# Single decay matrix in the delta-rule preparation, a block-by-block second half of the output projection, and modulation rows around the first attention steps

## The reference, cut to what matters

```python
mod = silu(c) @ w_mod + b_mod                       # 6 rows of 1024: shift, scale, gate, twice
h = rms_norm(x, pre_mix_gain) * (1 + scale_m) + shift_m
y = hybrid_mixer(h, ...)                            # proj = h @ w_in; two head groups; concat @ w_out
x = x + gate_m * rms_norm(y, post_mix_gain)
h = rms_norm(x, pre_ffn_gain) * (1 + scale_f) + shift_f
y = peer_ffn(h, ...)                                # product keys, top 16, 16384 experts
x = x + gate_f * rms_norm(y, post_ffn_gain)
```

```python
gdiff = g[:, None] - g[None, :]                     # g: cumulated log decay
decay = where(incl, exp(gdiff), 0)
L     = where(strict, (k * beta) @ k.T * decay, 0)  # strictly lower
sol   = triangular_solve(I + L, [v*beta, k*beta*exp(g)])
qk    = q @ k.T * decay
```

## Time and profile before

| | us |
|---|---|
| median of 3 runs | 1740.15 (1738.11 to 1740.58) |
| the profiled execution | 1740.75, span 1738.9 |
| PE busy | 1680.7, 97% of the span |
| DVE busy | 1245.3, 72% |
| POOL busy | 905.1, 52% |
| ACT busy | 701.5, 40% |

### The profile page before, as it was taken

One profiled execution on the slowest core, in us unless ns is written; L12 is line 12 of the kernel. 1 busy time (PEld: TensorE's weight loads), 2 busy tenths in 40 slices (PEclk: granted clock), 3 DMA queues, 4 the chain that ended last, 5 costly groups with the idle time before them and its releaser, 6 DMA issues.

```text
span 1738.9 us, 25635 instructions
## 1 busy us (share of the span) xinstructions
PE 1680.7 (97%) x7938; PEld 1393.7 (80%) x7938; DVE 1245.3 (72%) x3050; ACT 701.5 (40%) x1044; POOL 905.1 (52%) x710
## 2 busy tenths in 40 slices
PE   6999979987999999999999999999999999999997
PEld 5777769976888888888888888888888888888886
DVE  7658877584139999899899522223888888888886
ACT  5454565534233444444444444333333333333333
POOL 0232302043330177778777877761676776767730
PEclk9999989998999999999999999999999999999999
DMA  9422393353225644444444444466999999999993
GB/s 353 176 82 74 117 418 132 122 216 111 85 91 174 214 146 145 146 146 145 145 146 145 145 145 145 135 228 225 337 345 372 358 376 367 359 377 350 380 342 140
DMA packets 149363, 376.21 MB, mean 216 GB/s; under 512 B 32048, under 2 KB 64944, under 8 KB 146096
## 3 DMA queue, kind: packets, MB, share of 16 engines
q1 hardware_dynamic: 114480, 308.04, 50.0%
q0 software_dynamic: 34816, 67.41, 10.8%
HBM read 312.25 MB, written 63.11 MB: 216 GB/s over the span
## 4 chain that ended last, share of the span: by engine, by line
PE 90%; DVE 6%; ACT 2%; issue 1%; DVEq 1%; DMA 0%; SPq 0%; ACTq 0%
PE bank L1095 16%; PE bank L1096 16%; PE bank L1097 16%; PE bank L1494 10%; PE bank L1498 10%; PE bank L1496 10%; PE bank L1111 1%; PE bank L1113 1%; PE bank L1112 1%; PE bank L1295 1%; PE bank L1310 1%; PE bank L1454 1%; DVE modr L1568 1%; DMA xn<-in_x 0%; PE bank L1320 0%
## 5 line engine op out<-in xcount | busy, mean ns | idle before, releaser
L661 POOL DMA_INDIRECT gate_scratch<-merged,idx_cell x384 | 433.0, 1128 | 212.3 <-issue 125.3
L1095 PE MATMUL bank<-act_hi,whi 128*128 128x512 f32 x1312 | 514.5, 392 | 0.4 <-DVE act_lo L1590 0.4
L1096 PE MATMUL bank<-act_lo,whi 128*128 128x512 f32 x1312 | 511.1, 390 | 0.0
L1097 PE MATMUL bank<-act_hi,wlo 128*128 128x512 f32 x1312 | 511.1, 390 | 0.0
L1983 DVE TENSOR_TENSOR wlo<-raw,whi 128x1024 fp32r<-128x1024 f32 x254 | 309.9, 1220 | 180.2 <-ACT whi L1009 178.6
L1494 PE MATMUL bank<-whi,chi 128*128 128x512 f32 x768 | 298.8, 389 | 0.0
L1496 PE MATMUL bank<-wlo,chi 128*128 128x512 f32 x768 | 298.8, 389 | 0.0
L1498 PE MATMUL bank<-whi,clo 128*128 128x512 f32 x768 | 298.8, 389 | 0.0
L1095 PEld LDWEIGHTS bank<-act_hi,whi 128*128 128x128 f32 x1312 | 246.9, 188 | 51.6 <-DVE act_lo L1590 1.1
L1097 PEld LDWEIGHTS bank<-act_hi,wlo 128*128 128x128 f32 x1312 | 246.6, 188 | 51.5
L1096 PEld LDWEIGHTS bank<-act_lo,whi 128*128 128x128 f32 x1312 | 246.8, 188 | 50.1
(11 more groups left out here) (323 smaller groups left out, 1833.4 us busy)
## 6 DMA issues: line engine op xcount, KB each, us to landing
raw<-in_expert_tiles SPq DMA_DIRECT2D x256, 512.0 KB, 4.0
act_scratch<-aout SPq DMA_DIRECT2D x128, 256.0 KB, 2.1
gate_scratch<-zeros SPq DMA_DIRECT2D x24, 1024.0 KB, 22.4
a_in<-act_scratch SPq DMA_DIRECT2D x128, 192.0 KB
g_in<-gate_scratch SPq DMA_DIRECT2D x128, 192.0 KB, 7.0
raw<-in_in_tiles SPq DMA_DIRECT2D x28, 512.0 KB, 3.4
modr<-in_mod_tiles SPq DMA_DIRECT2D x16, 512.0 KB, 12.1
modz<-in_mod_tiles SPq DMA_DIRECT2D x16, 512.0 KB, 6.9
```

Of the source, the lines that this page charges most:

```text
L661: g.indirect_dma_start(out=gate_cells, out_offset=bass.IndirectOffsetOnAxis(ap=idx_cell[:, b, k:k + 1], axis=0), in_=merged[:, b, k:k + 1] ...
L1095: mm(out_bank[:], whi[:, slot, w], act_hi[:, k, :], start=(k == 0), stop=False)
L1096: mm(out_bank[:], whi[:, slot, w], act_lo[:, k, :], start=False, stop=False)
L1097: last = mm(out_bank[:], wlo[:, slot, w], act_hi[:, k, :], start=False, stop=(k == KD - 1))
```

## The change

Three parts.

1. Modulation rows 24 to 39 move to the front: 24 to 33 (`EARLY = 34`) right behind `gate_columns(0)`, then two in each of attention steps 0, 1 and 2, between biased(s) and difference(s). SP issues four rows ahead of each of tiles 8 to 13, with a wait only for the row that used the slot. The buffers `modz` are gone.
2. Delta-rule preparation: only `QKT` is built and passed through `Exp`; `a_products` multiplies it by the grams into `LM`, PE transposes that (`a_transposes`), and `first_level` multiplies by beta. The spread copy `gB` goes: PE reads the decay column as a broadcast operand. norm_sums(0..3) stand one tile earlier; the last V tile is copied by ACT to `state`, and its convolution stands behind the first masks. Four `qk_normed` stand in the first doubling steps.
3. Output projection: tiles 32 to 35 get slots of their own for every second pair, and their products run block by block: all 48 matmuls of block 0, then block 1, 2, 3. The chain of each block (root, gate, add, square, root, scale) follows on ACT and DVE; POOL adds nothing any more.

The names in the next two pieces: `modx`, `modr` are slots of modulation rows, `modcol` their results, `mrow` holds the lambda sums, `baT` the decay and beta columns.

The diff, cut to its core:

```diff
+EARLY = 34
...
-                if 26 <= m < 40:
-                    sp.wait_ge(s_uw, NB)
-                if 32 <= m < 40:
+                if 8 <= m < 40:
                     sp.wait_ge(s_modu, m - 7)
...
             for n in range(T_KQ, T_OUT):
-                for m in range(2 * n, min(2 * n + 2, 24)):
+                for m in range(4 * n - 16, min(4 * n - 12, 40)):
                     load_mod(m)
                 load_raw(n, in_tiles[n])
...
# DVE, start of attention
             gate_columns(0)
+            for m in range(24, EARLY):
+                mod_tile(m)
...
+                for m in range(EARLY + 2 * s, min(EARLY + 2 * s + 2, 40)):
+                    mod_tile(m)
...
# PE, preparation
-                if s == H * NB + 1:
+                if s == H * NB:
                     for n2 in range(4):
                         norm_sums(n2)
...
+            decay_rows(0)
             norm_sums(4)
...
+            decay_rows(1)
...
+            decay_rows(2)
+            norm_sums(5)
+            norm_sums(6)
+            pe.wait_ge(s_v3, 1)
+            decay_rows(3)
+            norm_sums(7)
...
# DVE, preparation
-                for out, m, ready in ((LM, M_NOT_STRICT, s_du[0]), (QKT, M_NOT_U, s_du[1])):
-                    for h in range(H):
...
+                for h in range(H):
+                    last = stt(out=QKT[:, t, h * HD:(h + 1) * HD], in0=row[:, h, :],
...
+            def a_products(t):
+                dve.wait_ge(s_kg, t + 1)
+                dve.wait_ge(s_de, t + 1)
+                tt(LM[:, t, :], QKT[:, t, :], bank[4 + t][:], ALU.mult).then_inc(s_A, 1)
+
+            def first_level(t):
+                dve.wait_ge(s_AT, t + 1)
+                tt(by_head(LM[:, t, :]), by_head(bank[t][:]), bc(g16(G_BETA), t), ALU.mult).then_inc(s_L, 1)
...
             first_masked(NB - 1)
+            dve.wait_ge(s_v3, 1)
+            conv(11)
+            v.drain()
+            v.memset(state[:], 0.0).then_inc(s_st, 1)
...
# PE, second half of the output projection
+            for b in range(NB):
+                for q in range(4):
+                    n = T_OUT + 4 + q
+                    h, l = out_weights(n)
+                    if b == 0:
+                        split_wait(n)
+                    for kk in range(2):
...
# DVE, behind it
+            for b in range(NB):
+                if b >= 1:
+                    x1_mean(b - 1)
                 block_mean(b)
+                y_by_gate(b, 1)
+                if b >= 1:
+                    x1_root(b - 1)
                 block_root(b)
+                stt(out=xn[:, b, :], in0=xs2[:, b, :], scalar=rstd[:, b:b + 1], in1=xn[:, b, :],
+                    op0=ALU.mult, op1=ALU.add).then_inc(s_x1[b], 1)
```

More of the change, by code:

```diff
@@ L841, in _ @@
                         sc.activation(l2r[:, n, :], qkvT[:, n, :], ACT.Square).then_inc(s_sq, 1)
-            for n in range(8):
-                act.wait_ge(s_l2, n + 1)
-                sc.activation(l2r[:, L2_ORDER[n], :], bank[SUM_BANK[n]][:], ACT.Ln,
-                              bias=eps_t).then_inc(s_l2r, 1)
+            for n in range(4):
+                norm_log(n)
+            act.wait_ge(s_used, T_OUT)
+            sc.copy(state[:], bank[1][:]).then_inc(s_v3, 1)
+            for n in range(4, 8):
+                norm_log(n)
             def inverse_norm(n):
@@ L854, in _ @@
             for t in range(NB):
-                act.wait_ge(s_du[0], t + 1)
-                sc.activation(LM[:, t, :], LM[:, t, :], ACT.Exp, scale=-1.0).then_inc(s_de, 1)
-            for n in range(4, 8):
-                inverse_norm(n)
-            act.wait_ge(s_du[1], NB + 1)
+                act.wait_ge(s_du, t + 1)
+                sc.activation(QKT[:, t, :], QKT[:, t, :], ACT.Exp).then_inc(s_de, 1)
+            act.wait_ge(s_du, NB + 1)
             for t in range(NB):
@@ L862, in _ @@
             last.then_inc(s_de, 1)
-            for t in range(NB):
-                sc.activation(QKT[:, t, :], QKT[:, t, :], ACT.Exp)
             sc.activation(g16(G_EXP), g16(G_CUM), ACT.Exp)
@@ L1342, in join_t @@
                 last.then_inc(s_tt, 1)
+            for t in range(NB):
+                a_transposes(t)
+            for t in range(NB):
+                first_transposes(t)
             for n in range(6 * NB + 1):
@@ L1733, in _ @@
             v.tensor_copy(g16(G_CUM), bank[7][:, 0:16]).then_inc(s_gcc, 1)
-            v.memset(state[:], 0.0).then_inc(s_st, 1)
             v.drain()
@@ L1738, in _ @@
                 row = by_head(bank[ROW_BANK[t]][:])
-                for out, m, ready in ((LM, M_NOT_STRICT, s_du[0]), (QKT, M_NOT_U, s_du[1])):
-                    for h in range(H):
-                        last = stt(out=out[:, t, h * HD:(h + 1) * HD], in0=row[:, h, :],
-                                   scalar=g16(G_CUM)[:, 4 * t + h:4 * t + h + 1], in1=masks[:, m, :],
-                                   op0=ALU.subtract, op1=ALU.add)
-                    last.then_inc(ready, 1)
+                for h in range(H):
+                    last = stt(out=QKT[:, t, h * HD:(h + 1) * HD], in0=row[:, h, :],
+                               scalar=g16(G_CUM)[:, 4 * t + h:4 * t + h + 1], in1=masks[:, M_NOT_U, :],
+                               op0=ALU.subtract, op1=ALU.add)
+                last.then_inc(s_du, 1)
                 tt(g16(G_DEC)[:, 4 * t:4 * t + 4], row[:, :, CH - 1], g16(G_CUM)[:, 4 * t:4 * t + 4],
@@ L1786, in first_masked @@
                 masked(t)
-            for n in range(6):
+            for n in range(4):
                 qk_normed(n)
+            for t in range(NB):
+                a_products(t)
             for t in range(NB):
@@ L1817, in _ @@
                 updated(n)
+                if n < 4:
+                    qk_normed(4 + n)
                 if n in QK_STEPS:
@@ L1903, in block_root @@
                 v.drain()
-            def y_gated(b):
-                for half in range(2):
-                    w = slice(half * 512, (half + 1) * 512)
-                    last = stt(out=xs2[:, b, w], in0=bank[4 * half + b][:], scalar=rstd[:, b:b + 1],
-                               in1=gate_m[:, w], op0=ALU.mult, op1=ALU.mult)
-                if b % 2 == 0:
-                    last.then_inc(s_yg, 1)
-            def x1_added(b):
-                v.drain()
-                tt(xn[:, b, :], xn[:, b, :], xs2[:, b, :], ALU.add).then_inc(s_x1[b], 1)
```

309 lines of the change are left out of this document (152 added, 157 removed).

## The result

The changed kernel takes 1745.5 us (median of 7 runs, 1743.6 to 1747.5), the kernel before 1740.5 (7 runs, 1737.7 to 1741.7): a ratio of 1.0029, 95% interval 1.0019 to 1.0039. It is 5.0 us slower, where I forecast 2.2, and the interval leaves out no change at all. The profiled executions differ by as much: 1745.86 against 1740.75.

What follows compares the result with a forecast made beforehand. PE works nearly without a gap, so time is won or lost only at its waits. 6.6 + 2.0 + 0.5 + 0.7 - 7.6 = +2.2 us, predicting 1742.4; range 1736 to 1749, the forecast's own 1739 to 1745.

Steps and rivals of the forecast that it cites:

- The new wait for `baT`: In front of tile 10, PE waits 6.6 us for DVE's copy behind ten rows; bounds 1.8 and 9.0.
- Rival A: Wait for `baT` only 1.8 us and the clock holds: 1735.6, faster; 0.13 together with a preparation that gains.
- The half clock behind it: After the wait for `baT`, PE restarts at half speed, costing 2.0 us; range 0 to 3.4.
- Two rows in steps 0 to 2: Two modulation rows on DVE in each of attention steps 0 to 2 cost 0.5 us; ends 0 and 4.1.
- The preparation, +0.7: Delta-rule preparation: grams start 1.3 us earlier, last transposes come 2.0 later, less that 1.3; bounds -2.5 and +3.5.
- Rival B: Half clock from grams to first doubling step costs +3.5, not +0.7: 1745.2; decides from 1.3 over; 0.41 with C.
- the +2.0, less 1.3 for the earlier start: Preparation: from grams' start to last transposes 16.4 us against 14.4, 2.0 later, less grams starting 1.3 earlier.
- It fills that hole exactly: Last V tile's convolution (3.2 us) and a memset (0.5) fill DVE's 3.62 us wait before PE's first doubling step.
- The output projection: Only block 3's chain remains behind the last matmul; PE's transposes start 8.8 us earlier; net -7.6, bounds -9.0 and -5.5.
- Given back: Behind the output projection, POOL's two consecutive remainders delay DVE's first `act_lo`, 1.2 us later against PE's start.
- Rival C: Chain behind the output projection's last matmul gives much less: -5.5, total 1744.5; 0.41 together with B.
- the side to which I gave 0.41: Whole kernel slower, by B or C, above 1743.6; same, from 1736.7 to 1743.6, had 0.46, faster 0.13.

Runs made afterwards that it cites:

- the short remainders: Changed kernel with GpSimd making the remainders of tiles 10 and 11 for only 16 of 1024 columns: 1740.2 us, ratio 0.9995 to the kernel before.
- the two rows fewer: Changed kernel with `EARLY = 32` for 34, rows 24 to 31 in front, two in each of steps 0 to 3: 1738.7 us, ratio 0.9990.
- the run with the copy first: Changed kernel with the lambda sums and the copy of `baT` again in front of rows 24 to 33: 1742.2 us, ratio 1.0013 to the kernel before.
- PE kept busy: Changed kernel with 20 unread matmuls of 512 columns on PE in front of its wait for `baT`: 1742.4 us, ratio 1.0015.
- without the early casts: Changed kernel, eight front rows, copy between rows 29 and 30, no twelfth-convolution wait, 20 unread matmuls before grams, V/K transposes one step later: 1732.3 us, ratio 0.9958.
- the late cast: The kernel without the early casts, with ACT's cast of tile 37 behind the eight pairs of h: 1732.1 us, ratio 0.9957 to the kernel before.

## Why the forecast was right in sign and short in size

**The new wait for `baT`**: right. 6.6 forecast, 5.98 measured; PE was free at 85.39 and the copy done at 91.3. Its three parts stand: 1.14 a row, 2.2 each for two rows beside GpSimd (shown by the short remainders and by the two rows fewer), early loads. The Trainium skill (SBUF — State Buffer, "SBUF: two separate sides") calls the shared port pair an exclusive lock that one instruction holds to its end. The rows of 3.42 and 3.37 us agree. GpSimd's 7.98 in the run with the copy first agrees in that the two never worked at once, but not in that the first to ask gets it: five rows passed while it stood. Rival A is out.

**The half clock behind it**: right, 2.0 forecast and 2.7 measured by PE kept busy; the other traces with this wait give 1.5 to 2.9, and in all of them the clock fell.

**Two rows in steps 0 to 2**: 0.5 forecast, nothing measured. In the four traces in which the copy stands between the rows and the scores come early, PE waits 0.51 to 0.53 us for the first of them.

**The preparation, +0.7**: the place and the path were right, the size was not. From the first scores to the last transposes the kernel before takes 159.57 us and this one 162.07; in the seven other traces with the same preparation it was 159.6 to 162.1. Up to 1.7 us of this spread lie in the attention's last step, where the clock fell or held behind the same wait of 2.39 us; it fell in the trace of the kernel before as in this one. So the kernels are compared from the cumulative sum on: 27.50 us before, 30.07 in this execution, 29.3 to 30.1 in the seven. The term is +1.8 to +2.6. Of its two parts the earlier start was mis-sized: the grams start 0.4 us earlier, counted from the first scores, where I had 1.3. The later end was nearly right: 16.4 us from the grams' start to the last transposes forecast, 17.3 here, 16.5 in the trace with the shortest, 14.4 before.

Rival B named the mechanism truly. It said that each product now stands behind four grams at half speed, and with the clock held by unread matmuls 2.1 to 2.9 us go. The half clock was as long in the kernel before (6.20 us for the grams), but there DVE waited only 0.96 for the first gram and then had work of its own; now it waits for all four, 4.8 us together, and 1.9 in front of the same four products where the clock held (without the early casts). So the change didn't make the grams slow, it put them on the path. My sum had them there too (the +2.0, less 1.3 for the earlier start); B's price of +3.5 was too high. With +1.8 to +2.6 the term lies about the line of +2.0 from which B was to decide. What the kernel before would win by faster grams, no run shows.

**"It fills that hole exactly"**, the convolution and memset behind the masks: this failed in its step, not in its price. They do fill DVE's hole, and DVE isn't what waits. But ACT's standing wait for the twelfth convolution was passed over. It costs 0.4 us, shown by its removal. From the last transposes to the products of `vbeta` the profiled execution took 65.27 us, and the seven other traces with this wait and this order 63.6 to 64.1. What made this execution 1.2 to 1.6 us longer stays open; its clock fell behind the 2.32 us of waiting, which is only a guess at the cause.

**The term that I didn't have**: `QK_STEPS` from (4, 5, 6, 7) to (5, 6, 7, 8). The prediction put the doubling at nothing and said nothing of it. The last decayed q k then stands on DVE in step 8 and the first V and K copies in step 9; PE waits 1.03 and 1.47 us there, 0.95 before. Moving V and K one step on wins 1.8 to 2.1 in the first run that has it and leaves 61.2 to 61.7 us in all three, against 61.31 before. So the four scalings that moved into the first steps, the other thing that is new in the doubling, cost little or nothing. `QK_STEPS` itself was not put back alone.

**The output projection**: right. -8.8 forecast for the chain of block 3 alone, -8.98 measured, of which 8.73 shown to be the block order. Given back: 1.2 forecast (its own two places, 396.3 and 403.6, give 1.5), 0.8 measured, and 0.8 shown by the late cast. Rival C is out.

So the 2.8 us between +2.2 and +5.0 are these: 2.3 to 2.8 in the doubling, which I had at nothing (about 2 for the steps, up to 0.4 for ACT's wait), and 1.1 to 1.9 in the preparation; against them 0.5 for rows that cost nothing and 0.6 in the output projection. The total also moves by 1 us and more with the clock, in the front and in the attention. The terms near 9 us, of both signs, each came within 0.3 us; what was missed were smaller ones, and the largest in a stage that I had called untouched. The measured total is near the 1745.2 of rival B, but only in part by B's doing: less than 2 us of the miss lie where B put 2.8. And by my own measure of 3.5 us for what can be told from no change, 5.0 us is slower and not the same: the side to which I gave 0.41, not the one with 0.46.

## What to carry to other kernels

Before work is put in an engine's idle time, look at which instruction behind it somebody else needs, and when: the hole was 12 us long, but the slack of the copy behind it was 8.85, and the repair was to put the copy in the middle of the work. Work added to one of two engines that share a port must be counted twice, for its own engine and for the other, in runs of few instructions so that neither is shut out for long. When something is moved, look at every wait of every engine for a count that it raises (here one `wait_ge(s_conv, 12)` from older code), and don't take a wait in the list for a loss: at half clock the same path took the same time with a wait of 0.2 us instead of 2.3. When the order of an engine's work is turned so that it waits for what it used to have in hand, look at how fast the other engine delivers: the grams ran at half clock before too, and most of it was hidden under DVE's work.

## What I had not expected of the hardware

- DVE and GpSimd: who gives way isn't fixed. In the changed kernel a row stood 2.2 us for GpSimd; with the copy first, five rows of 1.14 us ran one behind the other and GpSimd stood 5.6 us for all of them. Both times GpSimd came while a row was running. The second was seen once, in one trace; what decides it stays open.
- The same wait of PE didn't always have the same end. After a wait of 1.61 us the clock held in one run, after 1.53 it fell in another for some 3 us (7.62 instead of 6.02 to the scores). After the wait of 2.39 us in the attention's last step, which is in all fourteen traces, it fell in nine and held in five, and 1.7 us hung on it.
- Unread matmuls in a wait gave back 2.7 us in front and 2.1 to 2.9 in the preparation, for no cost while they were shorter than the wait.
- PE's same program reached the same point in the front up to 2.8 us apart (85.4 to 88.2), and from the first scores to the last values it took 128.8 to 131.1 us, by the clock of the norm sums at the end and by the 0.5 us of waiting in step 1. A difference of 2 us read from one trace of each kernel is within this; it has to be cut at PE's own marks first.
